# Two hybrid transformer blocks on one core: the second mixer with its x, B, C and dt chunks in reverse order

## The reference

```
proj = rmsnorm(h) @ w_in                       # 1024 -> 3344
q, k, v, z, xbc, dt = split(proj)              # 512, 128, 128, 1024, 1536, 16
attn = dilated_attention(rotary(q), rotary(k), v)          # 8 heads of 64
xbc  = silu(causal_depthwise_conv(xbc, conv_w, conv_b))    # 4 taps
xs, B, C = split(xbc)                          # 16 heads x 64, 2 groups x 128 each
dt = softplus(dt + dt_bias);  a = -exp(a_log) * dt;  cs = cumsum(a) in chunks of 128
y_diag = (C B^T * exp(cs_l - cs_s) for s <= l) @ (xs * dt)
y_off  = C @ (state of the chunk before) * exp(cs_l)
y = (y_diag + y_off + d_skip * xs) * silu(z)
y = rmsnorm over each of the 2 groups of 512, times ssm_norm
out = concat(attn, y) @ w_out                  # 1536 -> 1024
```

## Time and profile before

| | before |
|---|---|
| median of 3 runs | 1550.1 us |
| profiled execution | 1550.74 us, span 1549.0 us |
| busy in the span: TensorE, VectorE, ScalarE, GpSimd | 95%, 62%, 51%, 6% |
| instructions | 19412 |
| mean granted TensorE clock | 0.991 |
| DMA | 245.86 MB, mean 159 GB/s |

### The profile page before, as it was taken

How to read it: one execution, slowest core, us unless ns; L and a number is a source line. 1 busy time by engine, 2 the same in 40 slices (tenths; PEclk the granted TensorE clock), 3 DMA queues, 4 the chain that set the end, 5 groups by cost and what they waited for, 6 DMA issues and landing times.

```text
span 1549.0 us, 19412 instructions
## 1 busy us (share of the span) xinstructions
PE 1475.8 (95%) x7525; PEld 1258.3 (81%) x7525; DVE 957.6 (62%) x1352; ACT 782.3 (51%) x1226; POOL 88.5 (6%) x94
## 2 busy tenths in 40 slices
PE   4998999999999899999999999999999998999997
PEld 4887887888888788788888988788887987788886
DVE  4577775555466787555555697655555587755554
ACT  4575445444366634444444574544444575544442
POOL 0031200000000230000000010000000001000000
PEclk9999999999999999999999999999999999999999
DMA  6653264666465424466664343456554343455661
GB/s 210 215 169 108 82 190 155 200 190 189 141 216 159 145 82 136 149 199 205 187 187 122 113 146 100 148 189 203 188 183 140 110 146 109 150 174 181 190 191 54
DMA packets 180332, 245.86 MB, mean 159 GB/s; under 512 B 21008, under 2 KB 131984, under 8 KB 180240
## 3 DMA queue, kind: packets, MB, share of 16 engines
q1 hardware_dynamic: 180240, 244.61, 51.0%
HBM read 243.52 MB, written 1.05 MB: 158 GB/s over the span
## 4 chain that ended last, share of the span: by engine, by line
PE 79%; DVE 13%; ACT 5%; issue 2%; SPq 1%; DMA 0%; POOL 0%; POOLq 0%; DVEq 0%; ACTq 0%
PE acc L516 14%; PE acc L518 14%; PE acc L517 14%; PE misc L516 9%; PE misc L518 9%; PE misc L517 9%; DVE w_lo L1234 4%; PE misc L586 2%; DVE arena L1548 2%; ACT arena L948 1%; ACT w_hi L888 1%; PE misc L805 1%; PE misc L681 1%; PE misc L752 1%; DVE h_lo L1271 1%
## 5 line engine op out<-in xcount | busy, mean ns | idle before, releaser
L1234 DVE TENSOR_TENSOR w_lo<-w_raw,w_hi 128x1024 fp32r<-128x1024 f32 (+3 forms) x472 | 562.1, 1203 | 351.9 <-ACT w_hi L888 350.3
L888 ACT ACTIVATE w_hi<-w_raw 128x1024 fp32r<-128x1024 f32 (+3 forms) x472 | 480.2, 1028 | 308.5 <-PE misc L518 164.1
L516 PE MATMUL acc<-w_hi,h_hi 128*128 128x512 f32 (+3 forms) x832 | 314.0, 377 | 29.2 <-DVE h_lo L1271 29.2
L518 PE MATMUL acc<-w_hi,h_lo 128*128 128x512 f32 (+3 forms) x832 | 306.6, 368 | 0.0
L517 PE MATMUL acc<-w_lo,h_hi 128*128 128x512 f32 (+3 forms) x832 | 305.7, 367 | 0.0
L516 PE MATMUL misc<-w_hi,h_hi 128*128 128x512 f32 x640 | 253.3, 396 | 0.0
L518 PE MATMUL misc<-w_hi,h_lo 128*128 128x512 f32 x640 | 249.7, 390 | 0.0
L517 PE MATMUL misc<-w_lo,h_hi 128*128 128x512 f32 x640 | 249.2, 389 | 0.0
L516 PEld LDWEIGHTS acc<-w_hi,h_hi 128*128 128x128 f32 x832 | 159.2, 191 | 55.6 <-DVE h_lo L1271 33.0
L516 PE MATMUL acc<-w_hi,st_hi 128*128 128x512 f32 (+1 forms) x456 | 178.2, 391 | 0.0
L518 PEld LDWEIGHTS acc<-w_hi,h_lo 128*128 128x128 f32 x832 | 158.9, 191 | 22.3
(11 more groups left out here) (193 smaller groups left out, 1264.0 us busy)
## 6 DMA issues: line engine op xcount, KB each, us to landing
w_raw<-in_w_in SPq DMA_DIRECT2D x92, 512.0 KB, 4.5
w_raw<-in_w_gate SPq DMA_DIRECT2D x176, 256.0 KB, 2.9
w_raw<-in_w_up SPq DMA_DIRECT2D x176, 256.0 KB, 3.1
w_raw<-in_w_down SPq DMA_DIRECT2D x88, 512.0 KB, 3.6
w_raw<-in_w_out SPq DMA_DIRECT2D x40, 512.0 KB, 3.6
w_raw<-in_w_in SPq DMA_DIRECT2D x32, 388.0 KB, 3.3
w_raw<-in_w_in SPq DMA_DIRECT2D x16, 336.0 KB, 3.6
w_raw<-in_w_proj_a SPq DMA_DIRECT2D x8, 512.0 KB, 3.7
```

The costliest lines, as they stand in the source:

```text
L516: pe.matmul(dst, hi[:, k, cols], rhs_hi, start=first, stop=False)
L518: return pe.matmul(dst, lo[:, k, cols], rhs_hi, start=False, stop=last)
L888: act.activation(w_hi[:, g % RING, 0:w], w_raw[:, g % RING, 0:w], ACT.Copy)\
L1234: dve.tensor_tensor(w_lo[:, g % RING, 0:w], w_raw[:, g % RING, 0:w], w_hi[:, g % RING, 0:w].bitcast(F32), ALU.subtract)\
```

## The change

In the second mixer:

- The chunks are projected in the order xd3, xd2, xd1, xd0, so dt, C and B come first; the head pairs go 4 to 7, 0 to 3; z1 comes before z0. The slots of w_out take their row tiles in the order 0-3, 8-11, 4-7.
- The fourth tap with the bias moves from VectorE to ScalarE, as Identity with scale and bias out of PSUM in `channels`.
- log(dt) goes into the bias of the exponentials of the decays, so xs is no longer multiplied by dt on VectorE. The exponents of a pair are one minimum; the diagonal exponentials are four of 128 columns, each with a bias of its own.
- D·xs moves from GpSimd into VectorE's addition to y, now two scalar_tensor_tensor for a pair.
- The queues of ScalarE and VectorE are reordered. The first dt steps of VectorE (to dt_u) stand ahead of row_max(2); their Exp and Ln on ScalarE behind softmax(5).

```diff
@@ plan_b
+        ch[f"wo{i}"].slots = [(k, 2) for k in (0, 2, 8, 10, 4, 6)]
-        nT0 nT1 qkv0 nT2 nT3 qkv0 qkv1 qkv1 cvT0 cvT1 qkv2 qkv2 xd0 xd0 qkT0 qkT1 qkT2 qkT3 qkT4 xd0 S0 S1 xd0
-        xd1 PT0 S2 xd1 xT0 O0 PT1 S3 xd1 O1 PT2 S4 xd1 xd2 O2 PT3 S5 xd2 xT1 O3 PT4 xd2 xT2 O4 PT5 xd2 O5
-        xd3 attT0 attT1 xd3 xT3 xd3 xd3 z0 xT4 xT5 z0 z0 xsT0 xsT1 xsT2 xsT3 z0 z1 cb0 cb1 cs cr0 cr1
-        z1 y0 cr2 z1 y1 cr3 z1 y2 cr4 wo0 y3 cr5 wo0 y4 cr6 wo1 y5 cr7 ssT0 ssT1 wo1 y6 y7 wo0 wo0 wo1
-        ssT2 ssT3 wo1 wo0 wo0 wo1 mT0 mT1 wo1 mT2 mT3"""
+        nT0 nT1 qkv0 nT2 nT3 qkv0 qkv1 qkv1 cvT0 cvT1 qkv2 qkv2 xd3 xd3 qkT0 qkT1 qkT2 qkT3 qkT4 xd3 S0 S1 xd3
+        xd2 PT0 S2 xd2 xT5 O0 PT1 S3 xd2 O1 PT2 S4 xd2 xd1 O2 PT3 S5 xd1 xT4 O3 PT4 cs xd1 O4 PT5 xd1 O5
+        xd0 attT0 attT1 cr4 xd0 xT3 cr5 xT2 xd0 cr6 xd0 cb0 cb1 z1 xT1 xT0 z1 xsT1 xsT3 z1 z1 y4 cr7
+        z0 y5 cr0 xsT0 xsT2 z0 y6 cr1 z0 y7 cr2 z0 wo0 y0 cr3 wo0 y1 ssT2 ssT3 wo1 y2 wo1 y3
+        wo0 wo0 wo1 ssT0 ssT1 wo1 wo0 wo0 wo1 mT0 mT1 wo1 mT2 mT3"""
...
@@ ScalarE
 channels(i):
                                    ACT.Copy).then_inc(*AC.mark())
+                    if i == 5:
+                        act.wait_ge(*DV_.at(layer, "cvT1"))
+                    for k in (2 * i, 2 * i + 1):
+                        act.activation(cv[:, k, :], b[:, (k % 2) * T:(k % 2 + 1) * T], ACT.Identity,
+                                       scale=conv[:, 36 + k:37 + k], bias=conv[:, 48 + k:49 + k])\
+                            .then_inc(*AC.mark(f"xT{i}"))
...
+                def decays(hp):
+                    j = PAIRS.index(hp)
+                    b = wait_bank(layer, f"cr{hp}")
+                    act.wait_ge(*DV_.at(layer, f"cr{hp}"))
+                    E = Ex[j % 3]
+                    for u in range(2):
+                        hd = 2 * hp + u
+                        act.activation(E[:, u, P:2 * P], b[:, (2 * u + 1) * P:(2 * u + 2) * P], ACT.Exp,
+                                       bias=ncx[:, hd:hd + 1]).then_inc(*AC.mark(f"cr{hp}"))
+                    for u in range(2):
+                        hd = 2 * hp + u
+                        for part, bias in ((0, dt_v[:, hd:hd + 1]), (2, dt_v[:, 16 + hd:17 + hd])):
+                            v = E[:, u, part * P:(part + 1) * P]
+                            act.activation(v, v, ACT.Exp, bias=bias).then_inc(*AC.mark(f"ex{hp}"))
...
+                softmax(layer, 5, sc)
+                act.wait_ge(*DV_.at(layer, "dt_u"))
+                act.activation(dt_v, dt_v, ACT.Exp).then_inc(*AC.mark())
+                act.activation(ea, prm[:, 16:32], ACT.Exp).then_inc(*AC.mark())
+                act.wait_ge(*AC.now(layer))
+                act.activation(dt_v, dt_v, ACT.Ln, bias=1.0).then_inc(*AC.mark("dt_ln"))
+                channels(4)
+                act.wait_ge(*DV_.at(layer, "dt"))
+                act.activation(dt_v, dt_m, ACT.Ln).then_inc(*AC.mark("log_dt"))
+                turned_weights(layer, 4)
+                turned_weights(layer, 5)
+                mixed(1)
+                operand(layer, "attT0")
+                operand(layer, "attT1")
+                decays(4)
+                channels(3)
+                decays(5)
+                channels(2)
+                decays(6)
+                mixed(0)
+                conv_silu(2)
+                channels(1)
+                channels(0)
+                conv_silu(1)
+                turned_states(1)
+                turned_states(3)
+                conv_silu(0)
+                copy_product(layer, "z1", lambda t: zs[:, t, 512:1024], ACT.Silu, "x")
+                decays(7)
+                decays(0)
...
@@ VectorE
 convolve(i):
-                    for k in (2 * i, 2 * i + 1):
-                        dve.tensor_scalar(cv[:, k, :], xc[:, k, 3:3 + T], conv[:, 36 + k:37 + k],
-                                          conv[:, 48 + k:49 + k], ALU.mult, ALU.add).then_inc(*DV_.mark())
...
+                def exponents(hp):
+                    j = PAIRS.index(hp)
+                    b = wait_bank(layer, f"cr{hp}")
+                    if j >= 3:
+                        dve.wait_ge(*PE.at(layer, f"y{PAIRS[j - 3]}"))
+                    diagonal = Ex[j % 3].rearrange("p u (b t) -> p u b t", b=3)[:, :, 0:3:2, :]
+                    own = cs[:, 0:32].rearrange("p (t h a) -> p h t a", t=NT, a=1)[:, 2 * hp:2 * hp + 2, :, :]
+                    dve.tensor_tensor(diagonal, b[:, :].rearrange("p (u t q) -> p u t q", u=2, t=NT),
+                                      bc(own, [P, 2, NT, P]), ALU.min).then_inc(*DV_.mark(f"cr{hp}"))
...
+                row_max(layer, 5, sc)
+                weighed(layer, 3)
                 dve.wait_ge(*AC.at(layer, "dt_ln"))
-                dve.tensor_tensor(dt_m, dt_m, dt_v, ALU.add).then_inc(*DV_.mark("dt"))
+                dve.scalar_tensor_tensor(out=dt_m, in0=dt_u, scalar=1e-37, in1=dt_v, op0=ALU.max, op1=ALU.add)\
+                    .then_inc(*DV_.mark("dt"))
                 dve.wait_ge(*DV_.now(layer))
                 ea3 = bc(ea.rearrange("p (a h) -> p a h", a=1), [P, NT, 16])
                 dve.scalar_tensor_tensor(out=v3[3], in0=v3[1], scalar=-1.0, in1=ea3, op0=ALU.mult, op1=ALU.mult)\
                     .then_inc(*DV_.mark("dt_a"))
+                convolve(4)
+                weighed(layer, 4)
...
+                weighed(layer, 5)
+                operand(layer, "attT0")
+                operand(layer, "attT1")
+                split_until(layer, ORD[1].before["misc", "cr4"] + LOOK)
+                dve.wait_ge(*DV_.now(layer))
+                exponents(4)
+                convolve(3)
+                exponents(5)
+                convolve(2)
+                exponents(6)
...
+                convolve(1)
+                weighted_decays(4)
+                convolve(0)
+                weighted_decays(5)
+                weighted_decays(6)
+                exponents(7)
+                head_pair_out(4)
...
@@ GpSimd
-                for i in range(4):
-                    t, half = i // 2, i % 2
-                    pool.wait_ge(*AC.at(layer, f"xs{i}"))
-                    v = xs[:, t, 512 * half:512 * half + 512].rearrange("p (h d) -> p h d", h=8)
-                    dsk = prm[:, 32 + 8 * half:40 + 8 * half].rearrange("p (h a) -> p h a", a=1)
-                    pool.tensor_tensor(v, v, bc(dsk, [P, 8, SP]), ALU.mult).then_inc(*PO.mark("xsd"))
```

More of the change, by code:

```diff
@@ L255 @@
     {"attT0": ("st", 0, 2, 1.0), "attT1": ("st", 2, 2, 1.0),
-     **{f"ssT{i}": ("h", 2 * i, 2, 1.0) for i in range(4)}},
+     **{f"ssT{i}": ("h", (2 * i + 4) % KD, 2, 1.0) for i in range(4)}},
 )
@@ L1120, in conv_silu @@
                 def conv_silu(g):
-                    act.wait_ge(*DV_.at(layer, f"conv{2 * g + 1}"))
+                    act.wait_ge(*DV_.at(layer, f"conv{2 * g}"))
                     act.activation(cv[:, 4 * g:4 * g + 4, :], cv[:, 4 * g:4 * g + 4, :], ACT.Silu)\
                         .then_inc(*AC.mark(f"conv_silu{g}"))
[L1125 to L1155, removed]
@@ new lines, in body_b @@
+                softmax(layer, 0, sc)
+                softmax(layer, 1, sc)
+                mixed(3)
+                act.wait_ge(*DV_.at(layer, "pad"))
+                turned_weights(layer, 0)
+                softmax(layer, 2, sc)
+                channels(5)
+                turned_weights(layer, 1)
+                softmax(layer, 3, sc)
+                turned_weights(layer, 2)
+                softmax(layer, 4, sc)
+                mixed(2)
+                turned_weights(layer, 3)
+                softmax(layer, 5, sc)
@@ new lines, in body_b @@
+                turned_states(3)
[3 more added lines that the diff above has]
+                decays(0)
+                turned_states(0)
+                turned_states(2)
+                decays(1)
+                split_until(layer, ORD[1].before["misc", "cr2"] + LOOK)
+                group_squares(1)
+                decays(2)
+                copy_product(layer, "z0", lambda t: zs[:, t, 0:512], rms="x")
@@ L1191, in body_b @@
+                decays(3)
+                operand(layer, "ssT2")
+                operand(layer, "ssT3")
+                split_until(layer, ORD[1].before["misc", "y3"] + LOOK)
+                act.wait_ge(*AC.at(layer, "z0.t1"))
+                for t in range(NT):
+                    act.activation(zs[:, t, 0:512], zs[:, t, 0:512], ACT.Silu).then_inc(*AC.mark("z0_silu"))
+                group_squares(0)
                 operand(layer, "ssT0")
                 operand(layer, "ssT1")
-                split_until(layer, ORD[1].before["misc", f"y{SH // 2 - 1}"] + LOOK)
@@ L1194, in body_b @@
-                act.wait_ge(*AC.at(layer, "z1.t1"))
-                for t in range(NT):
-                    act.activation(zs[:, t, 512:1024], zs[:, t, 512:1024], ACT.Silu).then_inc(*AC.mark("z1_silu"))
-                group_squares(1)
-                operand(layer, "ssT2")
-                operand(layer, "ssT3")
```

(2 more changed lines are left out.)

163 lines of the change are left out of this document (65 added, 98 removed).

## The result

The changed kernel takes 1589.72 us (median of four runs, 1583.63 to 1590.66); the kernel before, run beside it, took 1550.19. The ratio is 1.0254 (1.0234 to 1.0274): 39.5 us slower, where 25 were forecast; the time lies 1.7 us above the upper end of the range, 1588. The profiled execution took 1589.5 us with a span of 1587.7 and a mean granted clock of 0.975 (0.991 before).

What follows compares the result with a forecast made beforehand. TensorE's work was taken as the bound, with VectorE limiting one stretch. New waits at cs and cb0 put mT0 12.8 us later; twice 12.6 is 25, and 1550.1 + 25 = 1575 us, range 1554 to 1588.

Steps and rivals of the forecast that it cites:

- The failed step: the clock: TensorE at half clock: 1.7 us a layer added behind cb0's wait, about 1.6 behind y0's old wait no longer lost.
- rival 4: The clock also falls behind the cs wait, up to 1.6 us a layer: 1578; counted inside the forecast's own range.
- cs wait: TensorE, free at 890.4, waits 5.1 us before the dt_a products, until VectorE delivers dt_a at 895.5.
- cs to the end of exponents(4): From cs through attention transposes and cr4 to VectorE's exponents(4), done at 907.6: 12.1 us.
- chain, exponents(4) to cb0: ScalarE and VectorE alternate without overlap up to conv_silu(2), so their links add up: 22.3 us, cb0 at 929.9.
- cb0 wait: TensorE reaches the B·C products at 915.7 and waits 14.2 us for conv_silu(2) on ScalarE.
- cb0 to mT0: TensorE's work from the B·C products to the mixer's end, 73.8 us plus clock 1.7 and xsT1 0.4: 75.9.
- The table between Ln and Exp: ScalarE loads a table, 1.28 us, before decays(4) behind the logarithm; without it the total is 2.6 us less.
- VectorE's queue as the limit of the old stretch: Before the change, VectorE, full from 911 to 927 us, causes TensorE's waits at cb0, cr1 and y0; some 8 us a layer.
- 1 (cb0 not late): Links to conv_silu(2) under about 9.7 us: about 1543 with the cs wait alone (0.07), 1534 with none (0.08).
- 2: The second wait, at cb0, is half the forecast size: 1555 to 1565; chance 0.09.
- Rival 3: Identity needs its own ScalarE table, four more loads of 1.28 us, 5 us a layer: 1585; chance 0.07.

Runs made afterwards that it cites:

- e9: Changed kernel with 20 matmuls of no use ahead of the cs wait and 60 ahead of the cb0 wait, per layer: 1578.26 us.
- e1: Changed kernel with cs three jobs later in TensorE's list and ScalarE's copy of PT4 ahead of the dt group: 1574.71 us.
- e2: Changed kernel with the ScalarE and VectorE queues reordered so that they no longer alternate, same instructions: 1577.02 us.
- e7: Kernel before with only D·xs moved from GpSimd into VectorE's addition to y: 1547.29 us, ratio 0.9983.
- e8: Kernel before, old order, with Identity tap, D in the addition, one minimum per pair and four biased exponentials; dt still multiplied on VectorE: 1546.10 us.
- e4: Changed kernel with cs later, helper queues no longer alternating, and conv_silu(2) ahead of decays(4): 1552.37 us.
- e12: e5 with matmuls of no use in its waits outside the second mixer's middle: 1542.81 us.
- e5: e4 with mixed(0) ahead of decays(6) on ScalarE: 1550.27 us, ratio 1.0000 to the kernel before.
- e6: Kernel before with only the fourth tap and bias moved to ScalarE as Identity: 1546.51 us, ratio 0.9988.
- e10: Kernel before with matmuls of no use ahead of its own short waits (norms, turned q and k, y0, feed-forward): 1539.62 us.

## Why the prediction was right about the mechanism and short in its size

**The failed step: the clock.** The sum had 1.7 us in a layer for it, behind cb0 only, and nothing behind cs or behind the norm after mT0; rival 4 allowed up to 1.6 behind cs. With the 1.6 at y0 taken off, the forecast had the clock costing no more than before. It costs 13.9 us more (25.7 against 11.8). Without the clock the two spans differ by 24.8 us, and the sum without its clock terms has 25.4, so the rest of it was sized right in total. The traces show, for layer (1,0):

| term, us in a layer | forecast | measured |
|---|---|---|
| cs wait | 5.1 | 4.89 |
| cs to the end of exponents(4), clock included | 12.1 | 15.6 |
| clock behind cs | 0 (rival 4: 1.6) | 3.3 (6.6 busy of 6.8 at half) |
| chain, exponents(4) to cb0 | 22.3 | 22.8 |
| cb0 wait | 14.2 | 15.14 |
| cb0 to mT0, clock included | 75.9 | 76.7 |
| clock behind cb0 | 1.7 | 2.9 (5.8 busy of 17.1 at half) |
| mT0 later by | 12.8 | 17.6 |
| clock behind the norm after mT0 | 0 | 1.7 (3.4 at half) |

The second row is 3.5 us longer than forecast, nearly all of it the clock; the chain adds 0.5 and the last stretch 0.8, and that is the 4.8 us by which mT0 comes later than forecast. Over the whole kernel the spans differ by 38.7 us: the changed kernel's trace is 1.1 us ahead when layer (1,0) begins, loses 17.6 to mT0, 1.6 from there to layer (1,1), 19.1 to that layer's mT0 and 1.5 behind it. The second layer loses more than the first because it also begins with a half-clock stretch (at 1211.6), which the kernel before does not have there. Clock that I had not put is then 3.3, 1.2 and 1.7 in each layer and 1.7 once, 14 us, against a forecast 14.5 us short.

The step took the earlier trace rows as the size of every fall: one stretch of about 3 us behind a wait of 1.65. It does not hold for these longer waits. With 4.89 us of waiting the half clock lasted 6.8 us, with 15.14 it lasted 17.1, to 5.8 us beyond the wait's end. e9 confirms it: the chains on the helpers are the same, the clock stays whole, its span is 10.1 us shorter, and its half clock costs 11.1 us less. That is the 12.4 of the two places in two layers less 1.3 which it costs more elsewhere (among it, stretches of 6.8 us at 122.3 and 238.4 in the first block, 3.4 in the changed kernel).

**cs.** Right: dt_a ended at 894.31, or 895.4 with the 1.1 us added, where the sum had 895.5, and TensorE stood for 4.9. That TensorE was free at 890.4 was partly luck: this is the start of PT4 before, whose row is 0.61 long. PT4 starts 0.4 us sooner in the changed kernel, so TensorE was free at 890.6. e1 took the wait away.

**cb0.** Right: ScalarE and VectorE take turns through 22.8 us, forecast 22.3. Single links came out off by tenths both ways (Identities 0.5 each, at the dear end of my bounds; four exponentials 1.2). e2 shows that the order costs: the same instructions, 12.7 us less, though 9.9 of the 15.1 us at cb0 stay.

**The table between Ln and Exp.** The load stands there, 1.28 at 910.09, so keeping it was right. The Trainium skill, "ScalarE: Activation LUTs", section "Table sets: the hidden batching unit", says that one set holds exp and ln, by which no load would stand there. The trace does not agree. No row shows which tables the loads at 890.33 and 910.09 brought. Rival 3 is out: ScalarE's timeline has no load at an Identity.

**VectorE's queue as the limit of the old stretch.** Only partly right. With GpSimd out of the way (e7) the waits at cb0 and half of cr1's went. But y0's 1.7 stayed through e7 and e8, though VectorE had idle time ahead of it in e8. I read one full stretch as the cause of three waits; one of them was latency. The changed kernel, with nearly the arithmetic of e8, has no such wait. I put that down to its order, y4 having several slots between it and its exponentials; no run shows this by itself.

**Rivals.** 1 (cb0 not late) is out by a wait of 15.1. 2 is out, since the chain took 22.8 and not about half. 4 was the right mechanism at half its size, and should have stood in the sum.

**Slips in the sum.** dt, B and C come at most three chunks earlier, not four. Five z slots at 2.84 make 14.2, not 13.9. Neither changes the total by more than 0.6 us.

What stays open: why the clock falls behind some waits and not behind others of the same length, so that the loss at places an edit doesn't touch moves by several us from kernel to kernel; and what e4 or e12 would take without the waits that their traces still name (xT1, then xsT1, near 4 us in a layer), since I ran no kernel without them. With its order mended the change gains nothing over parts of its arithmetic put into the old order: e5 stands 2 to 3 us behind e6 and e7 by the medians and ratios, about 1 us without the clock, which is hardly clear of the noise.

## What to carry to other kernels

Write the two helpers' queues side by side before reordering them: where every item of one needs the item just before in the other, the durations add, and what the third engine needs must not stand behind such a chain. Charge a wait of a nearly full TensorE with the half clock behind it as well (here 9.8 us of waiting at cs brought 6.6 us of lost clock), and compare kernels with the clock's loss counted apart, since it moves by some us at places that the edit doesn't touch. Then ask of a short wait whether the engine that ends it was busy or itself waiting; only the first gives way to less work.

## What the runs showed of the hardware

- The granted clock falls behind waits that the chain of the page hardly shows. Seven stretches at half clock of 3.4 us each stood in the kernel before; matmuls of no use ahead of four kinds of waits took all of them away and saved 10 us of 1550 (e10).
- A wait of 2.72 us after mT0 was followed by half clock in the changed kernel (last row of its stretches). Before the change a wait of 2.71 us at the same place was not:
```profile
996.00:999.40 3.40, 0.74 (x4) 0.28 (x2) 3.26 (x6) 1.17 (x2) 0.00 (x0) 1.00 0.24 73
999.40:1004.00 4.60, 4.55 (x24) 3.92 (x25) 2.09 (x4) 1.10 (x4) 0.00 (x0) 1.00 0.52 169
```
- The same holds within one trace. In the kernel before, the first product of layer (1,0) waits 2.19 us and that of layer (1,1) 2.21; the clock is at half behind the first alone. In the changed kernel it is at half behind the second too:
```profile
837.30:840.70 3.40, 3.40 (x16) 3.40 (x17) 1.63 (x4) 0.85 (x1) 0.83 (x2) 0.51 0.66 221
1193.60:1197.00 3.40, 3.38 (x28) 3.40 (x29) 1.67 (x4) 1.09 (x2) 0.87 (x2) 1.00 0.60 206
```
```profile
1211.60:1215.00 3.40, 3.27 (x15) 3.30 (x16) 1.79 (x4) 0.86 (x2) 0.89 (x2) 0.50 0.61 210
```
  So the length of the last wait does not settle alone whether the clock falls.
- GpSimd's multiplication of float32 made two VectorE subtractions of 128x1024 take 4.04 us instead of 2.35.
